# Hybrid decoder step on one core: ScalarE rounds the merge and w_o weights, GpSimd forms the token sum T3 in pieces

## What is computed

```
def merge_branches(o_att, y_conv, ga, gb, w_att_out, w_conv_out, w_o):
    ya = o_att.reshape(b, t, ATT_WIDTH) @ w_att_out
    yb = y_conv @ w_conv_out
    return (jax.nn.sigmoid(ga) * ya + jax.nn.sigmoid(gb) * yb) @ w_o
...
    x = x + gt1 * merge_branches(o_att, bgate * yc, ga, gb, w_att_out, w_conv_out, w_o)
    h2 = rms_norm(x, rms_g2) * (1 + sc2) + sh2
    x = x + gt2 * sqrelu_mlp(h2, w_mlp1, w_mlp2)        # square(relu(h2 @ w1)) @ w2
```

## Time and profile before

| what | value |
|---|---|
| median of 3 runs | 1663.25 us (1662.4 to 1663.83) |
| the profiled execution | 1661.66 us |
| its span in the trace | 1659.8 us |
| PE busy | 1612.9 us, 97% |
| DVE busy | 960.8 us, 58% |
| ACT busy | 447.8 us, 27% |
| POOL busy | 637.9 us, 38% |

### The profile page before, as it was taken

How to read it: one execution, slowest core, us unless ns; L and a number is a source line. 1 busy time by engine, 2 the same in 40 slices (tenths; PEclk the granted TensorE clock), 3 DMA queues, 4 the chain that set the end, 5 groups by cost and what they waited for, 6 DMA issues and landing times.

```text
span 1659.8 us, 31738 instructions
## 1 busy us (share of the span) xinstructions
PE 1612.9 (97%) x12312; PEld 1499.2 (90%) x12312; DVE 960.8 (58%) x1630; ACT 447.8 (27%) x802; POOL 637.9 (38%) x440
## 2 busy tenths in 40 slices
PE   7999999999999999999999998999999999999998
PEld 5898788878778878799999988999999999999998
DVE  5554364564544454437753689766666666666666
ACT  6344222222222322232111452222222222222220
POOL 0345143333334333413343226444444444444440
PEclk9999999999999999999999999999999999999999
DMA  9113346666656666534421100111111111111112
GB/s 384 41 44 98 145 161 223 214 204 217 201 177 235 218 232 215 167 130 170 157 103 51 39 26 26 52 52 52 52 52 52 51 52 52 52 52 52 52 39 105
DMA packets 71942, 194.74 MB, mean 117 GB/s; under 512 B 8018, under 2 KB 8147, under 8 KB 71795
## 3 DMA queue, kind: packets, MB, share of 16 engines
q1 hardware_dynamic: 67394, 178.62, 31.9%
q10 hardware_dynamic: 4400, 14.10, 2.3%
HBM read 174.26 MB, written 18.42 MB: 116 GB/s over the span
## 4 chain that ended last, share of the span: by engine, by line
PE 88%; DVE 5%; issue 2%; ACT 2%; POOL 1%; DMA 1%; SPq 0%; ACTq 0%; DVEq 0%; POOLq 0%
PE psum L809 74%; PE psum L934 2%; PE psum L959 2%; PE psum L947 2%; PE psum L983 2%; PE psum L1007 2%; PE psum L839 1%; POOL wl L710 1%; DMA pre<-in_weights 1%; DVE h2L L1805 1%; DVE rsq L1857 1%; POOL wh L708 1%; DVE sc L1837 1%; DVE act L1555 1%; PE psum L859 0%
## 5 line engine op out<-in xcount | busy, mean ns | idle before, releaser
L792 POOL TENSOR_TENSOR wl<-raw,wh 128x512 fp32r<-128x512 f32 x148 | 211.3, 1432 | 325.3 <-ACT wh L1409 325.3
L809 PE MATMUL psum<-hH,wh 128*128 128x352 f32 x832 | 276.5, 332 | 1.3 <-POOL wl L710 0.8
L809 PE MATMUL psum<-hL,wh 128*128 128x352 f32 x832 | 267.6, 322 | 0.0
L809 PE MATMUL psum<-hH,wl 128*128 128x352 f32 x832 | 267.0, 321 | 0.0
L809 PE MATMUL psum<-hidH,wh 128*128 128x352 f32 x768 | 248.5, 324 | 5.4 <-DVE act L1924 5.4
L809 PE MATMUL psum<-hidH,wl 128*128 128x352 f32 x768 | 248.0, 323 | 0.0
L809 PE MATMUL psum<-hidL,wh 128*128 128x352 f32 x768 | 247.8, 323 | 0.0
L735 POOL TENSOR_TENSOR beta<-beta,kb 128x512 f32<-128x512 f32 (+3 forms) x96 | 122.6, 1297 | 288.4 <-DVE kb L1607 288.4
L809 PEld LDWEIGHTS psum<-hH,wh 128*128 128x128 f32 x832 | 156.1, 188 | 28.4 <-issue 25.6
L1924 DVE SCALAR_TENSOR_TENSOR act<-psum,mods,act 128x352 f32<-128x352 f32 x256 | 145.3, 579 | 49.7 <-PE psum L809 49.5
L809 PE MATMUL psum<-h2H,wh 128*128 128x264 f32 (+1 forms) x544 | 159.7, 294 | 4.2 <-POOL wl L788 4.2
(11 more groups left out here) (239 smaller groups left out, 3341.0 us busy)
## 6 DMA issues: line engine op xcount, KB each, us to landing
raw<-in_weights SPq DMA_DIRECT2D x152, 512.0 KB, 3.6
ring<-in_cache_k SPq DMA_DIRECT2D x128, 256.0 KB, 3.9
ring<-in_cache_v SPq DMA_DIRECT2D x128, 256.0 KB, 3.6
pre<-in_weights SPq DMA_DIRECT2D x16, 512.0 KB, 16.2
gate_scratch<-gt ACTq DMA_DIRECT2D x14, 528.0 KB, 3.3
act<-gate_scratch SPq DMA_DIRECT2D x14, 528.0 KB, 4.8
xt<-in_xT SPq DMA_DIRECT2D x8, 528.0 KB, 7.0
act<-in_xT SPq DMA_DIRECT2D x8, 528.0 KB, 4.8
```

Source lines behind the costliest of these rows:

```text
L792: pool.tensor_tensor(xl, source_of(i), x.bitcast(F32), ALU.subtract).then_inc(S["split"], 1)
L809: mm = pe.matmul(out, x, y, start=n == 0, stop=n == end)
```

## The change

There are five edits.

1. `BY_ACT` now holds all units up to the MLP, so the high parts of the last 6 merge units and of the 8 w_o units (14 in all) are made by ACT (`split_high` in its merge and w_o loops) and no longer by GpSimd (L708).
2. In the first pair of the MLP, ACT makes the two high parts for pair 1 one group sooner: ahead of the evictions of groups 3 and 4, instead of behind those of groups 4 and 5.
3. T3 is formed on GpSimd, in four pieces of 528 elements: `t3(kt)` has three instructions a piece, two pieces ahead of halves 8, 9 and two ahead of halves 10, 11; `t3_low(kt)` has one a piece, ahead of half 12. VectorE's steps 6, 7, 8 and 10 go.
4. VectorE's low part of T2 and the steps of T4 stand earlier, and so do ScalarE's roundings of T3 and T4.
5. The last output block is written in three DMAs by chunk, not in one.

```diff
-BY_ACT = [*range(14, 42)]
+BY_ACT = [*range(14, PLAN.mlp0)]
...
-T_AT = {GROUP_OF["m1", 0, 0, 0] + 3 + n: n for n in range(9)}
-T_AT.update({GROUP_OF["m2", 0, d, 2]: n for d, n in ((0, 9), (2, 10), (4, 11), (6, 12))})
-T_AT.update({GROUP_OF["s", PLAIN, 0]: 13, GROUP_OF["s", PLAIN, 3]: 14})
-T_HIGH = {g: {2: 0, 4: 1, 8: 2, 13: 3}[n] for g, n in T_AT.items() if n in (2, 4, 8, 13)}
+T_AT = {GROUP_OF["m1", 0, 0, 0] + 3 + n: n for n in range(6)}
+T_AT.update({GROUP_OF["m1", 1, 1, 0]: 9})
+T_AT.update({GROUP_OF["m2", 0, d, 2]: n for d, n in ((1, 11), (4, 12), (7, 13))})
+T_AT.update({GROUP_OF["s", PLAIN, 3]: 14})
+T_HIGH = {g: {2: 0, 4: 1, 13: 3}[n] for g, n in T_AT.items() if n in (2, 4, 13)}
+T_HIGH[GROUP_OF["m1", 1, 1, 2]] = 2
...
+            for c in range(NCH):
+                sp.wait_ge(S["y_ready"], DB + c)
+                sp.dma_start(a["yT"][:, DB - 1, chunk(c)], act8[:, DB - 1, chunk(c)]).then_inc(S["y_out"], 16)
...
+            def t3(kt):
+
+                if kt == 0:
+                    pool.wait_ge(S["h2_lo"], NCH * DB + 1)
+                mark(pool.tensor_tensor(tf[2][:, kt, :], quarter(0, 1, 1)[:, kt, :].bitcast(F32),
+                                        quarter(0, 0, 1)[:, kt, :].bitcast(F32), ALU.subtract))
+                mark(pool.tensor_tensor(tu[2][:, kt, :], quarter(1, 1, 1)[:, kt, :].bitcast(F32),
+                                        quarter(1, 0, 1)[:, kt, :].bitcast(F32), ALU.subtract))
+                pool.wait_ge(S["pool_step"], steps[0])
+                pool.tensor_tensor(tf[2][:, kt, :], tf[2][:, kt, :], tu[2][:, kt, :], ALU.add).then_inc(S["t3_sum"], 1)
+
+            def t3_low(kt):
+                pool.wait_ge(S["t3_hi"], 1)
+                pool.wait_ge(S["t3_sum"], kt + 1)
+                pool.tensor_tensor(tL[2][:, kt, :], tf[2][:, kt, :], tH[2][:, kt, :].bitcast(F32), ALU.subtract).then_inc(S["t3_lo"], 1)
+
             for i, half in enumerate(HALVES):
+                if i in (8, 10):
+                    t3(i - 8)
+                    t3(i - 7)
+                if i == 12:
+                    for kt in range(4):
+                        t3_low(kt)
...
             for n, (b, c) in enumerate(MERGE_ORDER):
+                split_high(MERGE0 + 2 * n)
+                split_high(MERGE0 + 2 * n + 1)
...
             for n in range(20):
+                split_high(WO0 + n)
                 square2(n)
...
                 if GROUPS[g].kind == "m1":
+                    if g in (MLP0 + 3, MLP0 + 4):
+                        half_high(g + 1)
                     plain(g, g - MLP0)
...
-                half_high(g)
+                if g not in (MLP0 + 4, MLP0 + 5):
+                    half_high(g)
...
                 elif step == 11:
                     dve.wait_ge(S["dense_done"], GROUP_OF["m1", PLAIN - 1, 1, NCH - 1] + 1)
-                    dve.wait_ge(S["t_lo"], 3)
+                    dve.wait_ge(S["t_lo"], 2)
+                    dve.wait_ge(S["t3_sum"], 4)
```

More of the change, by code:

```diff
@@ L530, in program @@
             yc_in split_hi split_lo gate_in0 gate_in1 gate_in2 gate_in3 t1_done mix_add mix_hi mix_lo
-            x1_done squares2 rms2_done rstd2 scaled2 h2_hi h2_lo weight_sums t_sum t_hi t_lo hid_sq hid_hi hid_lo y_ready y_out
+            x1_done squares2 rms2_done rstd2 scaled2 h2_hi h2_lo weight_sums t_sum t3_sum t_hi t3_hi t_lo t3_lo hid_sq hid_hi hid_lo y_ready y_out
         """.split()}
@@ L674, in _ @@
                 load_raw(i)
-            for b in range(DB):
+            for b in range(DB - 1):
                 sp.wait_ge(S["y_ready"], b + 1)
                 sp.dma_start(a["yT"][:, b, :], act8[:, b, :]).then_inc(S["y_out"], 16)
-            sp.wait_ge(S["y_out"], 16 * DB)
+            for c in range(NCH):
+                sp.wait_ge(S["y_ready"], DB + c)
+                sp.dma_start(a["yT"][:, DB - 1, chunk(c)], act8[:, DB - 1, chunk(c)]).then_inc(S["y_out"], 16)
+            sp.wait_ge(S["y_out"], 16 * (DB - 1 + NCH))
             sp.wait_ge(S["vout"], 32)
@@ L1106, in winograd @@
                 split_done(i)
-                if p == PLAIN and PRODUCTS[j].tokens[0] == "T":
-                    pe.wait_ge(S["t_lo"], int(PRODUCTS[j].tokens[1]))
+                if p == PLAIN and PRODUCTS[j].tokens == "T3":
+                    pe.wait_ge(S["t3_lo"], 4)
+                elif p == PLAIN and PRODUCTS[j].tokens[0] == "T":
+                    pe.wait_ge(S["t_lo"], min(int(PRODUCTS[j].tokens[1]), 3))
                 release(g)
@@ L1411, in t_high @@
             def t_high(n):
-                act.wait_ge(S["t_sum"], n + 1)
+                if n == 2:
+                    act.wait_ge(S["t3_sum"], 4)
+                    act.activation(tH[n][:, :, :], tf[n][:, :, :], ACT.Copy).then_inc(S["t3_hi"], 1)
+                    return
+                act.wait_ge(S["t_sum"], min(n + 1, 3))
                 act.activation(tH[n][:, :, :], tf[n][:, :, :], ACT.Copy).then_inc(S["t_hi"], 1)
             for n in range(20):
+                split_high(WO0 + n)
                 square2(n)
+            split_high(WO0 + 20)
+            split_high(WO0 + 21)
             inverse2(0)
@@ L1924, in add_m2 @@
                     stt(x, ps[:, 0:CH], gate, x, ALU.mult, ALU.add).then_inc(S["bank_dve"], 1)
+                    if p == PAIRS - 1 and d == DB - 1:
+                        dve.wait_ge(S["bank_dve"], GROUPS[g].at)
+                        dve.sem_inc(S["y_ready"], 1)
                     return
@@ L1961, in token_sums @@
                     tt(tL[0][:, :, :], tf[0][:, :, :], f(tH[0][:, :, :]), ALU.subtract).then_inc(S["t_lo"], 1)
[L1962 to L1968, removed]
                 elif step == 9:
@@ L1986, in token_sums @@
                 else:
-                    dve.wait_ge(S["t_hi"], 4)
-                    dve.wait_ge(S["t_sum"], 4)
+                    dve.wait_ge(S["t_hi"], 3)
+                    dve.wait_ge(S["t_sum"], 3)
                     tt(tL[3], tf[3], f(tH[3]), ALU.subtract).then_inc(S["t_lo"], 1)
```

4 lines of the change are left out of this document (removed).

## The result

The changed kernel took 1666.83 us in the median of 8 runs (1663.91 to 1670.41), the one before 1663.15 (1662.21 to 1663.83): ratio 1.0024, 95% interval 1.0014 to 1.0033. It is slower by some 3.7 us. Timed a second time, beside the last experiments, it took 1665.54 (11 runs), the one before 1663.06 (27 runs): 1.0020, 1.0011 to 1.0029.

A forecast was written before the change was run, and what follows sets the result against it. TensorE, busy 1612.9 of 1659.8 us, was taken as the bound, so only its holes could be won. Terms -3.5 + 9.3 - 0.8 = +5.0 over 1663.25 gave 1668.2 us, range 1660.5 to 1672.5.

The forecast's parts named there:

- Edit 1, -3.5: Merge and w_o: rounding on ScalarE closes TensorE's small holes, 3.1 + 0.5 less 0.1, a gain of 3.5 us.
- Edit 2, 3.9 to 1 us, lost again: MLP's first hole: TensorE waits 1 us, not 3.9, but its lead turns into a wait in front of m2 0.
- Turn-taking in front of T1, +7.5: MLP pair 1: VectorE and GpSimd alternate on two-input instructions, T1's rounding 7.5 us later, 12 us wait before m2 0.
- The ninth group, +7 and 3 us: m2 0's ninth group: VectorE's first eviction comes 7 us later and TensorE waits 3 us.
- Product 2, +9.3: Product 2 starts 9.3 us later, behind GpSimd's queue up to S2's low part; this contains the delays before it.
- The Trainium skill's price: GpSimd two-input instruction: 4497 ns for 2048 elements, so a T3 piece 1.16 us and the sum about +3.3.
- The end, -0.8: Last output write in three transfers: 0.8 us gained, between 0.3 and 1.
- The likeliest case's upper edge: Whole kernel, 1671.5 us: pieces at 1.41 us and one more clock fall, adding 1.0 + 1.9.
- GpSimd doesn't yield: Rival for T3's pieces: GpSimd yields ties and pieces fill VectorE's idle stretches; total -1, 1662 us, chance 0.16.
- The pieces are not free: Rival for T3's pieces: they cost VectorE nothing and its chain is freed; total -8.6, 1654.6 us, chance 0.12.
- the third: Rival: gain ahead of the MLP doesn't come, or product 2 waits longer; +8.5, 1671.8 us, chance 0.10.

The follow-up runs named there:

- the table's third row: The changed kernel with edits 1 and 2 undone: 1669.07 us, ratio 1.0036 to the kernel before.
- its fifth and sixth: The changed kernel with edit 2 undone, timed twice: 1663.24 us and 1663.78 us.
- the memsets: The changed kernel with the first two of T3's four GpSimd pieces replaced by six memsets each, which read nothing: 1659.66 us.
- the second profile: Profiled execution of the unaltered changed kernel when timed again: 1665.08 us, with the median at 1665.54 us.
- the version at 1649.2 us: Kernel before plus edits 1, 2 and 5, ScalarE's T1 and T2 roundings later, VectorE's token sums re-placed, T3 on VectorE: 1649.21 us.
- the fastest kernel without edit 2: The version at 1649.2 us with edit 2 taken out: 1653.96 us, ratio 0.9943 to the kernel before.

## Why the prediction was right, and where it was off

It said slower, 1668.2 us by 5.0 us; measured were 3.7 and, the second time, 2.5 us, half of it. The mechanism held at the main steps; one term of the sum, product 2, was sized too large. Point by point, by its own steps:

1. **Edit 1, -3.5.** The marks say -3.8 in the change and alone, the medians -3.4 alone. Right, with its holes at 0.3 us. With T3 on GpSimd (the table's third row against its fifth and sixth, which differ by edit 1) the medians are 5.8 and 5.3 us apart, though the marks say -3.6; what makes up the rest stays open.
2. **Edit 2, 3.9 to 1 us, lost again.** Right: 0.99 us, and the clock stayed at 1.00 behind it, so TensorE had done pair 1 at 990.7 on the old clock, where 990.4 was forecast. Alone it gains nothing. What the text didn't see is that it makes edit 3 dearer: T1 is late by 7.1 us with it (two traces) and by 4.4 without (three).
3. **Turn-taking in front of T1, +7.5.** (The recorded steps, 986.6 less 979.2, make 7.4.) Measured +7.1 at T1's rounding, and +7.0 at m2 0, whose hole was 11.3 us where 12 were forecast. The mechanism is shown by the memsets. The forecast had the hole end with a low part by GpSimd; the trace names issue, but the low part ends 0.1 us ahead. That an eviction from PSUM doesn't wait is not in the row that the prediction names, where GpSimd is idle. It is in these two of the kernel before, where VectorE's two evictions take their 1.07 us inside GpSimd's half:

```profile
1010.22 2.36 POOL L792 TENSOR_TENSOR wl<-raw,wh 128x512 fp32r<-128x512 f32 x1 [8.51 <-ACT wh L1409]
...
1011.35 1.07 DVE L1924 SCALAR_TENSOR_TENSOR act<-psum,mods,act 128x352 f32<-128x352 f32 x2
```

4. **The ninth group, +7 and 3 us.** Measured +5.8 on the norm's clock and 2.83 us. T1's low part began 0.5 us sooner than forecast, and each row behind a piece was a little shorter than in the sum (the last four short ones 6.3 us for 6.7).
5. **Product 2, +9.3.** This is the term that was mis-sized: it started 7.1 us late. GpSimd ended T3's last addition at 1011.56, which is 1014.6 on the old clock, where 1016.3 were forecast, and the rest of its queue took 23.9 us and not 24.7. TensorE then waited 1.42 us, less than the 2 to 4 forecast, or 2.86 in the second profile; product 2 began at 1035.46 and 1035.48. It is GpSimd that sets this time, whatever TensorE lost before it: behind the ninth group's hole the clock was 0.52 from 1012 to 1015 us in the first profile and 1.00 in the second, and the 1.4 us that TensorE saved there it waited in front of product 2. The Trainium skill's price (GPSIMD Engine Reference, section 3.1) made a piece 1.16 us by the estimate and the sum 3.3, nearer to what was measured than mine. That nearness is luck: a piece that met nobody, the sixth of the change without edit 2, took 1.33 us, as I had it, and the forecast's chain holds sixteen pieces, which at 0.17 us less each make the sum 2.3, not 3.3:

```profile
983.29 1.33 POOL L794 TENSOR_TENSOR t3f<-t3f,t3u 128x528 f32<-128x528 f32 x1
```
6. **The end, -0.8.** Right: from VectorE's last instruction to the end of the span it is 2.3 us in each of the eleven traces with edit 5 and 3.1 to 3.2 in the three without.

With 7.3 in place of 9.3 for the MLP, and -3.8 and -0.75, the sum is +2.75, between the two measured differences. The rest of the first, 1 us, is within its interval. The likeliest case's upper edge comes to 1671.1 by the terms given for it (5.0, 1.0 and 1.9 over 1663.25), not 1671.5.

The rivals fell: GpSimd doesn't yield, as its pieces show at 1.6 us each beside a VectorE that had work all the time, and no idle stretch of VectorE was filled with them. The pieces are not free, with +4.7 to +7.4 us against +0.8 for memsets. The gain ahead of the MLP came, and product 2 didn't wait longer than forecast, so the third fell as well.

## What to carry to other kernels

Moving a two-input instruction from VectorE to GpSimd relieved neither here, as both had full queues: look for the stretch in which the partner is idle or evicts from PSUM, or move the work in time instead of across engines, as the version at 1649.2 us does. When a hole is closed, ask who is late behind it: edit 2 was worth nothing, cost some 2 us and was worth some 4 us in three kernels, by what stood behind it. An instruction that waits (here a rounding in front of ready evictions) should stand where what it waits for is about to be done.

## What the runs showed of the hardware

At 757 us the profiled executions lie up to 2.5 us apart, whatever the kernel, and the difference comes in three places. The first is the first 31 us, from -0.5 to +1.2 us against before. The second follows a hole of 1.77 us at 583 us that all have: behind it the granted clock stayed at 1.00 in nine of the fourteen traces and fell in five, at a price of 1.5 to 1.6 us. Here are the kernel before and edit 2 alone:

```profile
585.00:590.00 5.00, 5.00 (x35) 5.00 (x34) 1.80 (x6) 1.26 (x4) 0.90 (x2) 1.00 0.96 288
```

```profile
585.00:590.00 5.00, 5.00 (x23) 5.00 (x24) 1.11 (x4) 0.56 (x2) 0.90 (x2) 0.69 0.91 287
```

The third is a load from HBM that comes late by about 1 us at 615 us in seven of the executions (0.8 to 1.4 us), here in the changed kernel:

```profile
PE psum L1033 <- DMA ring<-in_cache_v: 1.1, 1, 1.1
```

That the clock after holes of the same length falls in one execution and not in another was shown at 583 us and in front of product 2 (1.5 and 1.4 us). Whether it also makes the scatter of the medians is open. The kernel with no hole over 1.5 us behind 780 us spread over 2.6 us in five runs and the changed one over 5.4 in eleven, but the fastest kernel without edit 2, which has a hole of 3.9 us there, spread over 0.9 in five, and the kernel before over 5.6 in 27. No profile caught one of the changed kernel's executions of 1668 us and more, so where those lose their time stays open.
